# Two tiles of a long float32 kernel moved from the start to the end of the on-chip memory

## The reference

```
h = x
for i in (0, 1):
    m = diff_attention(h) if i == 0 else short_gated_conv(h)
    h = layer_norm(ALPHA*h + m)
    h = layer_norm(ALPHA*h + silu(h @ w_gate) * (h @ w_up) @ w_down)
x = h
x = x + parallel_mixer(rms(x))          # mLSTM heads and stick-breaking heads
x = x + cross_attention(rms(x), rms(mem))
x = x + peer_ffn(rms(x))                # 16384 experts; 16 chosen per head, 8 heads
return rms(x)
```

## Time and profile before

| | |
|---|---|
| median of 3 runs | 1681.59 us |
| profiled execution, its own time | 1680.1 us |
| its span, first to last instruction | 1678.8 us |
| TensorE matmuls (PE) | 1659.8 us busy, 99% of the span, 11502 of them |
| weight loads (PEld) | 1514.1 us busy, 90% |
| VectorE (DVE), ScalarE (ACT), GpSimd (POOL) | 64%, 51%, 35% busy |
| mean DMA rate | 197 GB/s |

### The profile page before, as it was taken

The page is one execution under the profiler, slowest core; times in us unless marked ns, Lnnn a source line. Parts: engine busy times, 40 slices in busy tenths (PEclk is TensorE's granted clock), DMA queues, the critical chain, the costliest instruction groups (busy, mean ns, idle before and its releaser), DMA issues.

```text
span 1678.8 us, 29564 instructions
## 1 busy us (share of the span) xinstructions
PE 1659.8 (99%) x11502; PEld 1514.1 (90%) x11502; DVE 1072.6 (64%) x1812; ACT 862.1 (51%) x1291; POOL 594.7 (35%) x721
## 2 busy tenths in 40 slices
PE   9999999999999999999999999999999999999998
PEld 6788999899999989887889999999999988888887
DVE  6455555476655547645155789999999555555555
ACT  5586444344544436565444454454455555454554
POOL 0876000120300014555603665555555522222221
PEclk9999999999999999999999999999999999999999
DMA  9435555555555556242345677666566677777775
GB/s 346 150 140 176 189 189 187 189 202 178 210 188 177 199 176 215 103 173 101 130 172 179 205 223 218 204 202 203 177 186 180 220 244 237 246 240 241 243 242 194
DMA packets 97068, 330.55 MB, mean 197 GB/s; under 512 B 10988, under 2 KB 43020, under 8 KB 78368
## 3 DMA queue, kind: packets, MB, share of 16 engines
q1 hardware_dynamic: 94608, 320.64, 57.5%
q0 software_dynamic: 2032, 6.89, 1.3%
q10 hardware_dynamic: 288, 1.11, 0.2%
HBM read 310.26 MB, written 18.35 MB: 196 GB/s over the span
## 4 chain that ended last, share of the span: by engine, by line
PE 93%; DVE 3%; ACT 2%; DMA 1%; issue 1%; ACTq 0%; DVEq 0%
PE banks L1093 20%; PE banks L542 10%; PE banks L464 9%; PE banks L466 9%; PE banks L465 9%; PE banks L1056 7%; PE banks L1058 7%; PE banks L1057 7%; PE banks L492 4%; PE banks L1043 2%; PE banks L523 2%; PE banks L454 1%; DMA raw<-in_qkv 1%; DVE wL L1720 1%; PE banks L597 0%
## 5 line engine op out<-in xcount | busy, mean ns | idle before, releaser
L2488 POOL TENSOR_TENSOR wL<-raw,wH 128x256 fp32r<-128x256 f32 x312 | 239.5, 804 | 549.6 <-ACT wH L1129 540.4
L2264 DVE TENSOR_TENSOR uL<-raw,uH 128x512 fp32r<-128x512 f32 (+1 forms) x255 | 257.6, 1012 | 181.8 <-ACT uH L1622 181.1
L1622 ACT ACTIVATE uH<-raw 128x1024 fp32r<-128x1024 f32 x256 | 270.5, 1057 | 170.1 <-PE banks L1093 167.6
L464 PE MATMUL banks<-xH,wH 128*128 128x256 f32 x1168 | 329.3, 282 | 0.0
L466 PE MATMUL banks<-xH,wL 128*128 128x256 f32 x1168 | 328.7, 281 | 0.0
L465 PE MATMUL banks<-xL,wH 128*128 128x256 f32 x1168 | 328.7, 281 | 0.0
L2525 POOL TENSOR_TENSOR uL<-raw,uH 128x256 fp32r<-128x256 f32 x258 | 248.0, 981 | 226.1 <-ACT uH L1622 226.1
L1720 DVE TENSOR_TENSOR wL<-raw,wH 128x2048 fp32r<-128x2048 f32 (+1 forms) x102 | 231.2, 2271 | 130.1 <-ACT wH L1129 129.9
L1129 ACT ACTIVATE wH<-raw 128x2048 fp32r<-128x2048 f32 (+1 forms) x152 | 268.1, 1773 | 73.1 <-PE banks L542 66.8
L1056 PE MATMUL banks<-xH,uH 128*128 128x256 f32 x1024 | 294.0, 287 | 0.4 <-issue 0.4
L1058 PE MATMUL banks<-xH,uL 128*128 128x256 f32 x1024 | 288.1, 281 | 0.0
(11 more groups left out here) (387 smaller groups left out, 2719.2 us busy)
## 6 DMA issues: line engine op xcount, KB each, us to landing
raw<-in_eu SPq DMA_DIRECT2D x128, 512.0 KB, 3.7
raw<-in_ev SPq DMA_DIRECT2D x128, 512.0 KB, 3.5
raw<-in_gu SPq DMA_DIRECT2D x44, 1024.0 KB, 4.8
raw<-in_dn SPq DMA_DIRECT2D x22, 1024.0 KB, 4.8
gelu_scratch<-st SPq DMA_DIRECT2D x124, 128.0 KB, 3.6
st<-gelu_scratch SPq DMA_DIRECT2D x124, 128.0 KB, 3.4
raw<-in_win SPq DMA_DIRECT2D x14, 1024.0 KB, 4.9
raw<-in_cin SPq DMA_DIRECT2D x12, 1024.0 KB, 4.8
```

The source lines that it names most:

```text
L464: e.matmul(o, wh[:, w0:w0 + P], H[:, k, :], start=k == 0, stop=False)
L1622: e.activation(uH[n % US][:, :], raw[k // 2][:, (k % 2) * UW:(k % 2) * UW + UW], ACT.Copy).then_inc(s_uh, 1)
L2264: e.tensor_tensor(uL[n % US][:, c0:UW], raw[k // 2][:, (k % 2) * UW + c0:(k % 2) * UW + UW], uH[n % US][:, c0:UW].bitcast(F32), ALU.subtra ...
```

## The change

`xH` and `xL` take the last 16384 bytes below the usable end, rounded down to a multiple of 64. Everything that stood behind them moves down by 16384 bytes. No instruction, wait, transfer or shape is changed.

```diff
+    o = [nc.sbuf_usable_end // 64 * 64 - 2 * 4 * KT * S]
+    xH = sb("xH", [P, KT, S], F32R, off=o)
+    xL = sb("xL", [P, KT, S], F32R, off=o)
     raw = [sb(f"raw{i}", [P, CW]) for i in range(2)]
-    xH = sb("xH", [P, KT, S], F32R)
-    xL = sb("xL", [P, KT, S], F32R)
     ident = sb("ident", [P, P])
```

## The result

The changed kernel takes 1660.79 us (median of 4 runs, 1658.72 to 1664.02), beside 1681.9 for the kernel before (4 runs, 1680.54 to 1683.55): a ratio of 0.9878, 95% interval 0.9866 to 0.9889. That is 21 us faster, outside the range of 1670 to 1692 and on the other side of the forecast of 1685.3.

A forecast was written before the change was run, and what follows sets the result against it. The prediction took TensorE's matmuls to bound the kernel (busy 1659.8 of 1678.8 us). Adding 5.3 and giving back 1.6 made +3.7 us, so 1681.6 became a median of 1685.3 us, range 1670 to 1692.

The forecast's parts named there:

- the picture of the step: TensorE's matmul starts: aligned tiles fall into an even step, unaligned ones don't, costing time at 512 columns, gaining at 256.
- the rule of the Trainium skill: TensorE's two read ports are independent, so an address can't matter and the sum would be 0.
- The turned input as moving operand: 6744 matmuls with xH or xL moving, 0.78 ns more each: 5.3 us added.
- a ladder: Stationary-side steps at remainders 0, 192, 128 (226.7, 229.3, 232.9 ns) put 192 at 42%; moving step 119.45 ns.
- The lower bound: Best case for the moving term: 116 ns a matmul, from narrow stationary tiles, 2.7 ns less than before, -18 us.
- 1 in 50: Most chance given to gaining all 10 ns a moving matmul, down to the weight load's 109 ns: -65 us.
- As stationary operand: 432 matmuls with the turned input stationary, 3.6 ns less each as with eH: 1.6 us given back.
- The other tiles moved down: All other tiles 16384 bytes lower keep their remainders, so their steps stay: 0.
- The cover: If TensorE got much faster, VectorE and ScalarE would be next in line, between experts; a loss is hidden by nothing.
- The rival "faster": Pair loops and experts' first products: shorter 256-column steps at remainder 192, 117.0 ns, -13 us, 1668.7; chance 0.26.

The follow-up runs named there:

- e1: The changed kernel with xH and xL 64 bytes lower, back at remainder 128 modulo 256: 1680.89 us, ratio 1.000 to the kernel before.
- e2: The kernel before with two 32-byte tiles (mv, rs) put ahead of xH, giving it remainder 192 modulo 256: 1656.45 us, ratio 0.9857.
- e3: The kernel before with all four 32-byte tiles put ahead of xH, giving it remainder 0 modulo 256: 1687.23 us, ratio 1.004.
- e9: The kernel before with 64 free bytes and two 32-byte tiles ahead of xH, so the turned input is 192 above the weights: 1668.83 us.
- e10: e2 without the third of VectorE's gate products, TensorE reading the second one twice: 1651.05 us, ratio 0.9815 to the kernel before.
- e11: The changed kernel as it is, run again: 1660.12 us, ratio 0.9876 to the kernel before.

## Why the prediction was wrong

What was right is where the effect lies: the tiles' remainders modulo 256 against each other set which steps are possible. e1, e2, e3 and e9 show it. What was wrong is the picture of the step, that an aligned pair falls into an even one and no other pair does: with 192 between the tiles the starts are even too, and shorter (113.3 ns, durations of 276). By the rule of the Trainium skill, "TensorE: Matmul & The Clock Gate" (step on LDWEIGHTS), that the weight load takes nothing from the running matmul's reads, the prediction held that the time would stay; taken so, the runs don't agree with it, as a 64-byte shift of the turned input is worth 24 us (1656.45 against 1680.63). That it is these two reads that disturb each other was argued, and no run separates them. The sum failed at one term.

1. **The turned input as moving operand.** This is the step that failed. It was priced by a ladder: 42% of the way from 128 to 0 on the stationary side, carried over to the moving side, which made +0.78 ns and +5.3 us. Measured: -5.3 ns where the short rhythm holds. The term's size and its sign were wrong. The step isn't graded in the distance; by the table it goes 120.0, 116.7, 113.3, 120.0 in steps of 32 bytes. And 64 and 192 lie equally far from 0 and aren't the same on the stationary side (229.1 and 233.6). The lower bound was wrong too: the 116 ns of the narrow loads were taken for a floor, though the row with 109 ns lay below it and was put at 1 in 50. A nearest row of another form bounds nothing.
2. **As stationary operand.** Taken from eH, which had the same remainder: 229.3 foretold, 228.7 to 229.1 measured, 3.8 to 4.2 ns less each. The one term with a row of its own held.
3. **The other tiles moved down.** 0 foretold; last stage 354.0 and 354.1 us.
4. **The cover.** "If TensorE got much faster, the next in line would be VectorE" came true in the experts' first stage. At 5.3 ns for all 6744 matmuls and 1.6 us beside, 37 us were to be had, and the span fell by 20.4. Of the 16.3 us due in the experts' stage 2.8 came. The mean distance of two matmuls there, gaps over 260 ns left out, fell from 120.6 to 117.5 ns, so 9.5 us; 6.8 were kept by the longer rhythm in 37 of 128 experts (37 x 24 x 4.4 ns = 3.9 us), by the first steps of each, and by some 1.1 us of the stretch at half the clock. The other 6.7 went into gaps: 4.0 more for oA, 1.1 more in issue, some 0.6 of the same stretch, and 1.0 that has no name. e10 shows the first of these.

The rival "faster" had the right place and too small a price (-13, where 21 came); its chance was 0.26.

What stays open: what in the hardware makes the step depend on the distance, and what decides between 113.3 and 117.8 at a distance of 192 and of 64. It seems to be decided at the start of a sequence: the experts, which start anew 128 times, have both, e9's and e10's inner layers have one and the changed kernel's the other, and none of the long sequences (408 to 1056 matmuls) changes over on its way.

## What to carry to other kernels

Where TensorE is the bound and reloads its stationary operand for each matmul, read the distance between two starts for one form at different tiles, and work out their addresses: 64 bytes between the same tiles were worth 1.4% here. Try the distances (multiples of 32 modulo 256) on the chip, one use at a time, since what is best for 256 moving columns (192) isn't for 512 (0), and don't interpolate between them. Compare several executions, since one program can be in either rhythm. When the bound engine gets 4% faster in a stage, look at the wait that was 1.6 us before.

## What the runs showed of the hardware

- In this 32-bit matrix format a matmul of 256 moving columns with a weight load before each one took between 113.3 and 120.0 ns by the distance of the two tiles modulo 256, and one of 512 columns 226.7 ns or 229 to 234, with the granted clock at 1.00 in all these windows. At 2.4 GHz the even steps of 113.3, 120.0 and 226.7 ns are 272, 288 and 544 cycles, all multiples of 16.
- An uneven rhythm repeats too. In the kernel before, with 128 between the tiles, five starts take 593.3 ns (1424 cycles, again a multiple of 16), as 120, 119, 115, 118 and 122 to within 1 ns, in both inner layers.
- One program had executions of 1661.65 and 1671.77 us on one chip, the slower one at the higher mean clock (e9). One kernel ran one stage at 113.4 ns a matmul in one execution and at 117.8 in another (changed, e11).
